# Weighting an expert's output on its way out of PSUM and scattering it in two float32r passes

## The reference

```python
def moe_swiglu(h, router, w_gate_up, w_down):
    hf = h.reshape(bsz * seq, dm)
    logits = (hf @ router).astype(jnp.float32)
    top_v, top_i = lax.top_k(logits, TOP_K)              # 2 of 8
    gates = jax.nn.softmax(top_v, axis=-1)
    combine = jnp.sum(one_hot(top_i, N_EXPERTS) * gates[..., None], axis=1)
    for e in range(N_EXPERTS):
        out = out + combine[:, e:e + 1] * swiglu(hf, w_gate_up[e], w_down[e])
```

## Time and profile before

| | |
|---|---|
| runs | 1833.48, 1835.13, 1839.66 us |
| median | 1835.13 us |
| span of the profiled execution, first to last instruction | 1832.1 us |
| PE busy | 1691.4 us (92%) |
| DVE busy | 1394.0 us (76%) |
| ACT busy | 885.4 us (48%) |
| POOL busy | 221.6 us (12%) |
| mean granted TensorE clock | 0.973 |
| experts | from about 774 us to 1817 us of the span, some 130 us each |

### The profile page before, as it was taken

The page is one execution under the profiler, slowest core; times in us unless marked ns, Lnnn a source line. Parts: engine busy times, 40 slices in busy tenths (PEclk is TensorE's granted clock), DMA queues, the critical chain, the costliest instruction groups (busy, mean ns, idle before and its releaser), DMA issues.

```text
span 1832.1 us, 22620 instructions
## 1 busy us (share of the span) xinstructions
PE 1691.4 (92%) x8124; PEld 1345.0 (73%) x8124; DVE 1394.0 (76%) x1328; ACT 885.4 (48%) x731; POOL 221.6 (12%) x386
## 2 busy tenths in 40 slices
PE   6778999999797899899999999999999999999995
PEld 5556858888675685677777777787778778787774
DVE  8897356454557835598889888888898898888886
ACT  1002124333100111377667677676676676676673
POOL 5481029200028200000000000000000000000000
PEclk9888999999898899999999999999999999999998
DMA  8422185545232225499999999899899999999991
GB/s 286 149 77 71 68 282 183 184 162 182 92 115 70 69 92 203 165 327 364 332 332 348 337 334 353 303 348 361 310 358 328 330 361 334 326 363 330 327 363 68
DMA packets 217707, 457.39 MB, mean 250 GB/s; under 512 B 7910, under 2 KB 60167, under 8 KB 216888
## 3 DMA queue, kind: packets, MB, share of 16 engines
q1 hardware_dynamic: 216888, 451.96, 70.2%
q0 software_dynamic: 768, 4.75, 0.7%
HBM read 454.06 MB, written 2.62 MB: 249 GB/s over the span
## 4 chain that ended last, share of the span: by engine, by line
PE 84%; DVE 11%; issue 3%; ACT 1%; POOL 0%; DMA 0%; SPq 0%; POOLq 0%; DVEq 0%; ACTq 0%
PE psum L487 19%; PE psum L489 18%; PE psum L488 18%; PE psum L532 6%; PE psum L677 3%; PE psum L692 3%; PE psum L494 2%; PE psum L496 2%; PE psum L495 2%; PE psum L843 2%; DVE arena L1417 1%; PE psum L866 1%; PE psum L575 1%; PE psum L558 1%; PE psum L656 1%
## 5 line engine op out<-in xcount | busy, mean ns | idle before, releaser
L304 DVE TENSOR_TENSOR wl<-ring,wh 128x2048 fp32r<-128x2048 f32 x379 | 867.9, 2298 | 212.5 <-ACT wh L299 211.7
L299 ACT ACTIVATE wh<-ring 128x2048 fp32r<-128x2048 f32 x379 | 728.7, 1923 | 261.3 <-PE psum L489 159.2
L487 PE MATMUL psum<-wh,xgh 128*128 128x512 f32 x896 | 356.8, 398 | 4.8 <-issue 1.7
L489 PE MATMUL psum<-wh,xgl 128*128 128x512 f32 x896 | 349.6, 390 | 0.0
L488 PE MATMUL psum<-wl,xgh 128*128 128x512 f32 x896 | 348.8, 389 | 0.0
L487 PE MATMUL psum<-wh,hidh 128*128 128x512 f32 x536 | 215.7, 402 | 23.2 <-issue 20.3
L532 PE MATMUL psum<-xT,ring 128*128 128x256 f32 (+1 forms) x896 | 205.3, 395 | 12.4 <-DMA ring<-in_w_in 11.5
L489 PE MATMUL psum<-wh,hidl 128*128 128x512 f32 x536 | 209.3, 390 | 0.0
L488 PE MATMUL psum<-wl,hidh 128*128 128x512 f32 x536 | 208.9, 390 | 0.0
L532 PEld LDWEIGHTS psum<-xT,ring 128*128 128x128 f32 (+1 forms) x896 | 166.2, 191 | 52.2 <-issue 23.0
L487 PEld LDWEIGHTS psum<-wh,xgh 128*128 128x128 f32 x896 | 168.3, 188 | 43.5 <-DVE wl L304 4.9
(11 more groups left out here) (260 smaller groups left out, 1750.7 us busy)
## 6 DMA issues: line engine op xcount, KB each, us to landing
ring<-in_moe_gu SPq DMA_DIRECT2D x224, 1024.0 KB, 5.9
ring<-in_moe_dn SPq DMA_DIRECT2D x112, 1024.0 KB, 5.6
ring<-in_w_in SPq DMA_DIRECT2D x26, 1024.0 KB, 5.3
ring<-in_w_gu SPq DMA_DIRECT2D x22, 1024.0 KB, 5.0
ring<-in_w_dn SPq DMA_DIRECT2D x11, 1024.0 KB, 4.9
ring<-in_w_out SPq DMA_DIRECT2D x8, 1024.0 KB, 5.0
ring<-in_w_pg SPq DMA_DIRECT2D x8, 1024.0 KB, 4.9
lnp<-in_ln POOLq DMA_DIRECT2D x4, 1024.0 KB, 7.3
```

The lines of the kernel that those rows point to most:

```text
L299: eng.activation(wh[:, u % SPLIT, :], ring[:, u % RING, :], ACT.Copy).then_inc(hi_ready, 1)
L304: eng.tensor_tensor(wl[:, u % SPLIT, :], ring[:, u % RING, :], wh[:, u % SPLIT, :].bitcast(F32), ALU.subtract).then_inc(lo_ready, 1)
L487: pe.matmul(dst, ah, bh, start=first, stop=False, skip_group_check=True)
L489: return pe.matmul(dst, al, bh, start=False, stop=last, skip_group_check=True)
```

## The change

The gate is no longer in `spread`. At L1141 ScalarE now makes two things of the transposed `pickw`: by Identity with an accumulated sum the column `slot_gate`, the gate of each slot, and by Sign the zero-one matrix `spread` in float32r. `ye` becomes two float32r tiles: ScalarE writes `yeh`, the expert's output times `slot_gate`, rounded; VectorE writes `yel`, output times `slot_gate` minus `yeh`. The scatter multiplies `spread` with `yeh` and then with `yel`, each product into the same bank, so it has eight products in place of four. TensorE waits for both subtractions of VectorE ahead of it. On VectorE the subtractions stand behind the split of ("u", 1), ahead of the additions.

```diff
--- before.py
+++ after.py
@@ -147,10 +147,12 @@
         hid = overlay("hid", [P, 2, 512])
         xgh = overlay("xgh", [P, KD, P], F32R)
         xgl = overlay("xgl", [P, KD, P], F32R)
-        ye = overlay("ye", [P, D])
+        yeh = overlay("yeh", [P, D], F32R)
         pick = overlay("pick", [P, 2, P])
         pickw = overlay("pickw", [P, 2, P])
-        spread = overlay("spread", [P, 2, P])
+        spread = overlay("spread", [P, 2, P], F32R)
+        slotw = overlay("slotw", [P, 2, P])
+        yel = overlay("yel", [P, D], F32R)
         rl = overlay("rl", [NE, SEQ])
         topi = overlay("topi", [P, NB, 8], U32)
         assert over[0] <= arena_at
@@ -217,6 +219,7 @@
         topf = small[:, 32, 8:24].rearrange("p (a b) -> p a b", a=2)
         gts = sm(35, 6, 20)
         cnt = sm(36, 2, 12)
+        slot_gate = sm(36, 1, 28)
 
         psum = ctx.enter_context(nc.psum_tensor("psum", [P, 8, 512], F32))
         bank = [psum[:, i, :] for i in range(8)]
@@ -264,7 +267,7 @@
         pick_ready, x_free = sem("pick_ready"), [sem("slot_bank5_free"), sem("slot_bank6_free")]
         x_full, xg_ready, hT_ready, spread_ready = sem("slot_group_full"), sem("gathered_ready"), sem("hiddenT_ready"), sem("spread_ready")
         spread_full, outer_added = sem("spread_out_full"), sem("expert_out_added")
-        ye_full, ye_ready = sem("expert_out_full"), sem("expert_out_ready")
+        ye_full, ye_hi, ye_lo = sem("expert_out_full"), sem("expert_out_hi_ready"), sem("expert_out_lo_ready")
 
         block = ctx.enter_context(nc.Block())
 
@@ -913,14 +916,19 @@
                 if not last:
                     project(1, 0, order_ahead[("g", 1)], it)
 
-                pe.wait_ge(ye_ready, it + 1)
-                pe.wait_ge(spread_ready, it + 1)
+                pe.wait_ge(ye_lo, 2 * it + 2)
+                pe.wait_ge(spread_ready, 2 * it + 2)
+
+                def scatter(dst, b, o):
+
+                    part = slice(o * 512, (o + 1) * 512)
+                    pe.matmul(dst, spread[:, b, :], yeh[:, part], start=True, stop=False)
+                    return pe.matmul(dst, spread[:, b, :], yel[:, part], start=False, stop=True)
+
                 for o in range(2):
-                    pe.matmul(slot_group(x + 1 + o, it)[:, :], spread[:, 0, :], ye[:, o * 512:(o + 1) * 512],
-                              start=True, stop=True).then_inc(x_full, 1)
+                    scatter(slot_group(x + 1 + o, it)[:, :], 0, o).then_inc(x_full, 1)
                 for o in range(2):
-                    pe.matmul(bank[2 + o][:, :], spread[:, 1, :], ye[:, o * 512:(o + 1) * 512],
-                              start=True, stop=True).then_inc(spread_full, 1)
+                    scatter(bank[2 + o][:, :], 1, o).then_inc(spread_full, 1)
 
             gather(0, None, 1)
             pe.wait_ge(xg_lo, 2)
@@ -1138,9 +1146,10 @@
                 two_hi(order[("d", 0)], it)
                 hidden_tanh(1, it)
                 two_hi(order[("g", 2)], it)
-                act.activation(spread[:], slot_group(1, it)[:, 0:2 * P].rearrange("p (a b) -> p a b", a=2),
-                               ACT.Copy).then_inc(spread_ready, 1)
-                act.wait_ge(spread_ready, it + 1)
+                turned = slot_group(1, it)[:, 0:2 * P].rearrange("p (a b) -> p a b", a=2)
+                act.activation(slotw[:], turned, ACT.Identity, accum_out=slot_gate).then_inc(spread_ready, 1)
+                act.activation(spread[:], turned, ACT.Sign).then_inc(spread_ready, 1)
+                act.wait_ge(spread_ready, 2 * it + 2)
                 act.nop().then_inc(x_free[1], 1)
                 for j in range(2, ESTEPS):
                     if j > 2:
@@ -1161,8 +1170,8 @@
                     hidden_tanh(0, it + 1)
                     two_hi(order_ahead[("g", 1)], it)
                 act.wait_ge(ye_full, it + 1)
-                act.activation(ye[:, 0:512], bank[2][:, :], ACT.Copy)
-                act.activation(ye[:, 512:1024], bank[3][:, :], ACT.Copy).then_inc(ye_ready, 1)
+                for o in range(2):
+                    act.activation(yeh[:, o * 512:(o + 1) * 512], bank[2 + o][:, :], ACT.Copy, scale=slot_gate).then_inc(ye_hi, 1)
                 if not last:
                     two_hi(order[("u", 1)], it + 1)
 
@@ -1639,6 +1648,11 @@
                     two_lo(order[("u", 1)], it + 1)
 
                 for o in range(2):
+                    part = slice(o * 512, (o + 1) * 512)
+                    dve.wait_ge(ye_hi, 2 * it + o + 1)
+                    dve.scalar_tensor_tensor(out=yel[:, part], in0=bank[2 + o][:, :], scalar=slot_gate, in1=yeh[:, part].bitcast(F32),
+                                             op0=ALU.mult, op1=ALU.subtract).then_inc(ye_lo, 1)
+                for o in range(2):
                     g = x + 1 + o
                     dve.wait_ge(x_full, it * SLOT_GROUPS + g + 1 + EARLY)
                     part = xa[:, 0, o * 512:(o + 1) * 512]
```

## The result

The changed kernel takes 1863.48 us (median of four runs, 1863.12 to 1864.20) against 1835.27 us (the three runs of before and a fourth, 1835.40): a ratio of 1.0144, 95% interval 1.013 to 1.0158, 28.2 us slower. The profiled execution took 1863.12 us, with a span of 1861.2 us, 29.1 us more than before.

What follows compares the result with a forecast made beforehand. The prediction took the expert loop to run at TensorE's pace, 92% busy. Terms of 13.0 (seam waits), 0.5 (last expert) and 8.0 us (clock) made +21.5 on 1835.1: 1856.6 us, range 1845 to 1864.

Steps and rivals of the forecast that it cites:

- Part 1: Scatter between experts: eight float32r products take 1.92 us against 3.44 before, saving 1.5 us an expert if operands are there.
- rival 3: Wait at the seam does not decide, subtractions finish before TensorE arrives: full saving of 12.2 us, 1823 us; chance 0.06.
- Part 2: ScalarE's two scaled copies out of PSUM at the seam: +0.1 us each, 0.2 us for both, passed to VectorE's chain.
- Part 3: VectorE's two subtractions at the seam take 1.39 us; TensorE waits 3.2 us, +1.86 us a seam, +13.0 us in seven.
- Part 4: Last expert, where no split stands in the way: +0.5 us, bounds 0 and 1.
- one of the signs: Waits of TensorE for VectorE's subtraction: seven times 3.2 us, once under 1 us.
- Part 5: Selection at L1141: Identity with sum plus Sign add 0.4 to 0.5 us on ScalarE, eight times, covered: 0.
- rival 4: Sign at L1141 needs another table, a load of 1283 ns: +8 us on top of the forecast, 1865; chance 0.03.
- Part 6: TensorE's clock behind the seam waits: five falls of seven, 1.6 us lost a time, +8.0 us.
- Rival 2: Clock falls at every seam: 1859.8 us, chance 0.17; with twice the length 1871, a further 0.03.
- Rival 1: Wait comes at the seams but the clock stays high or falls once or twice: 1848.6 us; chance 0.22.
- Rival 5: Wait at the seam is just the size of the saving, VectorE's split running some 1.5 us earlier: 1835 us; chance 0.04.

Runs made afterwards that it cites:

- twelve idle products: Changed kernel with 12 products whose result is overwritten and never read put into TensorE's wait at each seam between experts; 1851.16 us, ratio 1.008.
- the last kernel: The kernel "both early" with the first half of the scatter sent to banks 0 and 1, so VectorE hands back 5 and 6 earlier; 1825.96 us, ratio 0.9932.
- four, at full clock: Changed kernel with 4 idle products in TensorE's wait, here its two seams without a clock fall; kernel 1858.92 us, ratio 1.0113.
- both early: Changed kernel with VectorE's two subtractions moved ahead of the split of ("u", 1); 1831.22 us, ratio 0.9973.
- high part alone: Changed kernel without VectorE's subtractions and the four products with yel, TensorE waiting for ScalarE alone; 1831.54 us, ratio 0.9969.

## Why the prediction was right, and where it was short

The forecast was slower, 1856.6 us; the time is 1863.48, half a microsecond below the upper end of the range. The mechanism came as told: the wait, its cause in VectorE's order, its direct cost and the low clock behind it. What was short is the number of falls, at the seams and outside them.

**Part 1.** 1.92 us for eight float32r products: 1.95 us at full clock with twelve idle products ahead (1055.71 to the transposes at 1057.66). Right. In the changed kernel itself, at half the clock, they took 3.47 us at the second seam (1058.66 to 1062.13). That the saving is 1.5 us "if the operands are there" is right too, but only the last kernel has it; see rival 3.

**Part 2.** The scaled copies take 684 ns, 0.09 us more each, and the split begins 1.16 us behind the first copy in place of 0.97 us (1049.60 to 1050.76): the +0.2 us of the text.

**Part 3.** A subtraction takes 744 ns and the pair 1.40 us; 1.39 was worked out. Lines by form of the changed kernel:

```profile
L1174 ACT ACTIVATE yeh<-psum,small 128x512 fp32r<-128x512 f32 x16 | 10.1, 684 | 14.1 <-PE psum L492 14.1
L1653 DVE SCALAR_TENSOR_TENSOR yel<-psum,small,yeh 128x512 fp32r<-128x512 f32 x16 | 11.2, 744 | 8.2 <-ACT yeh L1174 8.2
```

The wait is 3.12 us for 3.2, the direct cost of a seam 1.75 us (twelve idle products) or 1.86 us (four, at full clock) for 1.86, in seven 12.2 to 13.0 us for 13.0. That is the distance from seam to seam, so nothing was caught up behind the wait and little or nothing was lost there.

**Part 4.** From ScalarE's first copy to VectorE's first statistics the kernel before takes 5.68 us (1811.40 to 1817.08), the one with both subtractions early, whose end is that of the changed kernel at full clock, 6.10 us (1806.82 to 1812.92): +0.4 for +0.5. TensorE's wait there is 2.3 us and not under 1, as one of the signs had it; TensorE had waited 1.3 us for the copies in the kernel before too.

**Part 5.** Nothing was expected, and no wait of TensorE shows at ("u", 2). Identity, accumulator read and Sign took their time on ScalarE; VectorE's idle time ahead of the split of ("u", 2) grew from 1.21 us in the earlier trace rows to 1.58 us, and the cover held. Timeline of the changed kernel at that place:

```profile
1074.64 0.38 ACT L1150 ACTIVATE slotw<-psum 128x256 f32<-128x256 f32 x1 [1.01 <-PE psum L898]
1074.92 0.19 ACT L1150 ACTIVATION_READ_ACCUMULATOR slotw<-psum 128x1 f32 x1
1075.01 0.38 ACT L1151 ACTIVATE spread<-psum 128x256 fp32r<-128x256 f32 x1
...
1077.53 4.50 DVE L307 TENSOR_TENSOR wl<-ring,wh 128x2048 fp32r<-128x2048 f32 x2 [1.58 <-ACT wh L302]
```

Sign follows the accumulator read without a table load between them, so rival 4 is out.

**Part 6** is the term that was mis-sized. Five falls at 1.6 us, 8.0 us; it was seven, one of them of twice the length, 11.3 to 12.1 us. The mechanism was right and a single row carried it; taking a share of it in place of the whole cost 3 to 4 us. Rival 2, a fall at every seam, gave 1859.8, and is the case that came; the falls outside the seams, below, make up most of the 3.7 us to the measured time. Rival 1, no falls, is what the twelve idle products made: 1848.6 by the text, 1851.16 measured. The Trainium skill, "TensorE: Matmul & The Clock Gate", section on HAM oscillation, tells of a wait of some 3 to 5 us at each step, after which each group starts at the low clock; the changed kernel's trace agrees, with waits of 3.1 us, seven of seven.

Two falls outside the seams, at 789.1 and 1833.7, stood in no part of the sum: 1.6 us each. The waits ahead of them are in the kernel before as well, with the clock kept. Both stand in unchanged work. Of the other kernels some have one or both falls and some none, with nothing changed at those places, so they are not shown to be an effect of the change. Together: 24.3 at the seams + 2 x 1.6 + 0.4 = 27.9 us of the 28.2.

**Rival 3** put the gain without the wait at the whole 12.2 us, 1823 us, and the turning point at a wait of 1.5 us. The size was wrong. The text had noted that the transposes need bank 5 back from VectorE's first addition, and called it just in time; with the scatter 1.5 us shorter and at its old place it is no longer in time, and 0.8 us a seam is all there is: 1831.2 us. My expectations for the kernels "both early" and "high part alone" made the same mistake. The gain of rival 3 comes only in the kernel with other banks: 1825.96 us against 1838.21 beside it, with seams 1.55 us shorter, which makes 10.9 us of the 12 in seven. **Rival 5**, a wait just as long as the saving, is out: the wait is 3.12 us and the saving 1.5.

**What stays open.** Why the clock fell at all seven waits of 3.1 us in the changed kernel, and at three of seven of 2.9 us with plain products, has not been settled.

## What to carry to other kernels

A product made of two operands has to wait for the later one, so look first at where its producer stands in its engine's order, and what stands ahead of it there: here the same work placed 4.5 us earlier in VectorE's order turned a loss of 28 us into a gain of 5 (ratio 0.9973). Price a stop of TensorE twice, once for its length beyond what is saved and once for the low clock that may follow it. When a wait is removed, ask what comes next to be late (here the return of a bank), before the saving is counted in full.

## What the runs showed of the hardware

The clock fell more readily than I had expected from the kernel before: at 5 of 7 stops of 2.1 us, 6 of 7 of 2.5 us, 7 of 7 of 3.1 us, but 3 of 7 of 2.9 us with plain float32 products behind the stop, and none of 7 of 1.5 us. The two stops of 1.7 to 1.9 us that every one of the nine kernels has in unchanged places, at the first expert's second unit and in the last expert, were followed by a fall in 11 of 18 cases. So the length of the stop alone does not say whether it falls. At the seams it stayed low each time for 3.4 or 6.7 us. Products whose result nobody reads, put into the stop, kept it at 2.4 GHz at all seven seams, and the kernel was 12 us faster (1851.16 against 1863.48).
